# A fused two-block transformer kernel: the mLSTM takes the two heads of a pair together, with a score bank each, and the dense products beside the mixers keep to two banks

## The reference, cut to what matters

```
h = rmsnorm(x, norm1_g[l])
u = jnp.einsum('btd,de->bte', h, w_in[l])
(mq, mk, mv, mo, mi, mf, aq, ak, av, hq, hf, hi, hg) = jnp.split(u, split_at, axis=-1)
y_m = mlstm_mixer(mq, mk, mv, mo, mi, mf, mlstm_conv_w[l], mlstm_gate_b[l], mlstm_norm_g[l])
y_a = diff_attention(aq, ak, av, diff_q_norm_g[l], diff_k_norm_g[l], diff_lambda[l], diff_subln_g[l], lambda_init)
y_h = hgrn2_mixer(hq, hf, hi, hg, lower_bounds[l], hgrn_norm_g[l])
mix = jnp.concatenate([y_m, y_a, y_h], axis=-1).astype(x.dtype)
x = x + jnp.einsum('bte,ed->btd', mix, w_out[l])
```

```
S = jnp.einsum('bhtd,bhsd->bhts', qb, kb) * jnp.exp(D - m_t[..., None])
num = jnp.einsum('bhts,bhsv->bhtv', S, vb) + scale[..., None] * jnp.einsum('bhvk,bhtk->bhtv', C, qb)
den = jnp.sum(S, axis=-1) + scale * jnp.einsum('bhk,bhtk->bht', n, qb)
h = num / jnp.maximum(jnp.abs(den), jnp.exp(-m_t))[..., None]
```

## Time and profile before

| | us |
|---|---|
| median of three runs | 3792.15 |
| lowest and highest | 3792.1, 3793.68 |
| the profiled execution | 3790.01 |
| its span, first to last instruction | 3788.7 |
| mean granted TensorE clock | 0.934 of full |
| PE busy | 3443.1 (91%) |
| DVE, ACT, POOL busy | 1360.0, 1133.6, 1221.5 |

### The profile page before, as it was taken

How to read it: one execution, slowest core, us unless ns; L and a number is a source line. 1 busy time by engine, 2 the same in 40 slices (tenths; PEclk the granted TensorE clock), 3 DMA queues, 4 the chain that set the end, 5 groups by cost and what they waited for, 6 DMA issues and landing times.

```text
span 3788.7 us, 36989 instructions
## 1 busy us (share of the span) xinstructions
PE 3443.1 (91%) x15506; PEld 2733.4 (72%) x15506; DVE 1360.0 (36%) x2212; ACT 1133.6 (30%) x1553; POOL 1221.5 (32%) x300
## 2 busy tenths in 40 slices
PE   7887899998976999999997789998999979769998
PEld 5654588886744788888886678886888857547887
DVE  4437531314257421222126541224221253573123
ACT  2234342322134332322222232223222233422222
POOL 4210044443200244434442234443444431014442
PEclk9887799999978899999998899999999989869998
DMA  3110033332200133333332223323433322013332
GB/s 121 60 52 1 12 100 100 93 96 68 78 19 1 56 100 93 96 100 89 101 86 73 86 67 92 108 89 111 125 93 106 84 97 84 1 39 91 98 96 71
DMA packets 462182, 296.75 MB, mean 78 GB/s; under 512 B 14330, under 2 KB 454192, under 8 KB 462016
## 3 DMA queue, kind: packets, MB, share of 16 engines
q1 hardware_dynamic: 453664, 277.09, 25.0%
q10 hardware_dynamic: 8352, 17.30, 1.3%
HBM read 285.97 MB, written 8.39 MB: 78 GB/s over the span
## 4 chain that ended last, share of the span: by engine, by line
PE 82%; DVE 14%; ACT 3%; issue 1%; POOL 0%; SPq 0%; DMA 0%; ACTq 0%; DVEq 0%
PE bank L473 24%; PE bank L474 24%; PE bank L475 24%; PE bank L313 9%; DVE ta L525 1%; DVE x L750 1%; DVE ta L748 1%; DVE ta L1132 1%; DVE xl L773 1%; DVE qkv L1914 0%; DVE u L1428 0%; DVE ta L1911 0%; DVE scr L1669 0%; DVE sqacc L767 0%; DVE tb L1912 0%
## 5 line engine op out<-in xcount | busy, mean ns | idle before, releaser
L413 POOL TENSOR_TENSOR wlo<-raw,whi 128x2048 fp32r<-128x2048 f32 (+3 forms) x288 | 1209.1, 4199 | 2530.0 <-ACT whi L406 2530.0
L473 PE MATMUL bank<-xh,whi 128*128 128x512 f32 x2432 | 973.6, 400 | 70.4 <-DVE xl L773 39.4
L474 PE MATMUL bank<-xl,whi 128*128 128x512 f32 x2432 | 960.0, 395 | 0.0
L475 PE MATMUL bank<-xh,wlo 128*128 128x512 f32 x2432 | 959.3, 394 | 0.0
L406 ACT ACTIVATE whi<-raw 128x2048 fp32r<-128x2048 f32 (+3 forms) x288 | 503.5, 1748 | 685.6 <-PE bank L475 650.7
L473 PEld LDWEIGHTS bank<-xh,whi 128*128 128x128 f32 x2432 | 465.1, 191 | 187.1 <-POOL wlo L413 33.2
L475 PEld LDWEIGHTS bank<-xh,wlo 128*128 128x128 f32 x2432 | 464.4, 191 | 99.2
L474 PEld LDWEIGHTS bank<-xl,whi 128*128 128x128 f32 x2432 | 465.6, 191 | 93.8
L473 PE MATMUL bank<-ah,whi 128*128 128x512 f32 x1216 | 473.0, 389 | 0.0
L474 PE MATMUL bank<-al,whi 128*128 128x512 f32 x1216 | 473.0, 389 | 0.0
L475 PE MATMUL bank<-ah,wlo 128*128 128x512 f32 x1216 | 473.0, 389 | 0.0
(11 more groups left out here) (333 smaller groups left out, 3046.1 us busy)
## 6 DMA issues: line engine op xcount, KB each, us to landing
raw<-in_ffn_w_gate SPq DMA_DIRECT2D x88, 512.0 KB, 4.0
raw<-in_ffn_w_up SPq DMA_DIRECT2D x88, 512.0 KB, 5.2
raw<-in_w_up SPq DMA_DIRECT2D x64, 512.0 KB, 4.7
raw<-in_w_down SPq DMA_DIRECT2D x64, 512.0 KB, 5.2
raw<-in_w_in SPq DMA_DIRECT2D x56, 512.0 KB, 4.7
raw<-in_ffn_w_down SPq DMA_DIRECT2D x64, 384.0 KB, 4.1
raw<-in_ffn_w_down SPq DMA_DIRECT2D x64, 320.0 KB, 3.7
raw<-in_w_out SPq DMA_DIRECT2D x16, 512.0 KB, 4.4
```

The costliest lines, as they stand in the source:

```text
L413: g.e.tensor_tensor(self.wlo[slot][:, 0:n], self.raw[slot][:, 0:n], self.whi[slot][:, 0:n].bitcast(F32), ALU.subtract).then_inc(self.lo_ma ...
L473: pe.e.matmul(bank, hi[:, at:at + P], xh, start=k == ks[0], stop=False)
L474: pe.e.matmul(bank, hi[:, at:at + P], xl, start=False, stop=False)
L475: last = pe.e.matmul(bank, lo[:, at:at + P], xh, start=False, stop=k == ks[-1])
```

## The change

In the mLSTM the two heads of a pair are taken together. Both `weigh`s of the pair run first; then each b step makes the score blocks of both heads in turn (one on rows 0 to 63 of the array, one on rows 64 to 127) into a bank each (2 and 4), DVE multiplies both, and TensorE sums both. The number of products, of DVE operations and of exponentials stays as it was; the number of steps of the line falls. Nothing of the next pair's `weigh` runs ahead any more. Since bank 2 is now the mLSTM's, the dense units of `in_ah` and `out` all use banks 0 and 1, and TensorE waits, before it begins a bank, until DVE has taken the previous unit's tile out of it. The first unit of each `up` phase also waits for the tiles of the unit before it. hgrn always has banks 0 and 1, `heads(0)` banks 2, 3 and 4.

```diff
+    def two_banks(self, ph):
+        return ph.name.startswith("in_ah") or ph.name.startswith("out")
+
+    def dense_banks(self, u):
+        return 0 if self.two_banks(UNITS[u]) else 2 * (u % 2)
...
+            if u and ph.name.startswith("up") and j == 0:
+                pe.wait_ge(self.tile_read, self.tile_read[u - 1])
...
+                if k == ks[0] and self.two_banks(ph):
+
+                    pe.wait_ge(self.tile_read, self.tile_read[(u - 1, t) if UNITS[u - 1].tiles else u - 1])
                 at = k * w + t * P
-                bank = self.bank[2 * slot + t][:]
+                bank = self.bank[banks + t][:]
...
-        s_bank, row_bank, *sum_banks = [self.bank[b] for b in (4, 5, 6, 7)]
+        row_bank, s_banks, sum_banks = self.bank[5], [self.bank[b] for b in (2, 4)], [self.bank[b] for b in (6, 7)]
...
             elif h == 2:
-                pe.wait_ge(a, a["weights", l, 1])
+                pe.wait_ge(a, a["below", l, 0])
             else:
-                pe.wait_ge(a, a["tokens", l, h // 2])
+                pe.wait_ge(a, a["weights", l, h - 1])
...
             for j in range(b + 1):
-                last = self.mm(s_bank[:, j * P:j * P + P], self.u[part, MK + i, j * P:j * P + P],
-                               self.u[part, MQ + i, b * P:b * P + P], j == 0, j == b)
-            last.then_inc(done.tick("scores", l, h, b), 1)
-        run(weigh(0))
+                for e in range(2):
+                    part = slice(e * HD, e * HD + HD)
+                    last = self.mm(s_banks[e][:, j * P:j * P + P], self.u[part, MK + i, j * P:j * P + P],
+                                   self.u[part, MQ + i, b * P:b * P + P], j == 0, j == b)
+            last.then_inc(done.tick("scores", l, i, b), 1)
         for i in range(2):
             vt = sp(8), sp(9)
-            pe.wait_ge(a, a["below", l, 0] if i else a["weights", l, 0])
+            if i:
+                yield
+            yield from weigh(2 * i)
+            yield from weigh(2 * i + 1)
+            pe.wait_ge(a, a["weights", l, 2 * i + 1])
...
+            scores(i, 0)
+            yield
+            for b in range(NB):
+                yield
+                if b + 1 < NB:
+                    scores(i, b + 1)
...
-            yield from hgrn((mine, mine + 1))
+            yield from hgrn((0, 1))
...
-            yield from weave((heads(0, (2 - mine, 3 - mine, 4)), 1), (line, 1))
+            yield from weave((heads(0, (2, 3, 4)), 1), (line, 1))
```

More of the change, by code:

```diff
@@ L440, in pe_dense @@
         for j in range(ph.count):
-            u, slot = ph.first + j, (ph.first + j) % 2
+            u, slot, banks = ph.first + j, (ph.first + j) % 2, self.dense_banks(ph.first + j)
             pe.wait_ge(self.lo_made, self.lo_made[u])
@@ L453, in pe_dense @@
             if ph.tiles == 0:
-                bank = self.bank[2 * slot]
+                bank = self.bank[banks]
                 for k in range(KC):
@@ L555, in dve_dense @@
                 read = self.tile_read.tick(u, t)
-                self.dve_tile(ph, j, t, self.bank[2 * (u % 2) + t], read)
+                self.dve_tile(ph, j, t, self.bank[self.dense_banks(u) + t], read)
             self.tile_read.tick(u, by=0)
@@ L1047, in pe_mlstm @@
             last.then_inc(done.tick("tokens", l, i), 1)
+            pe.wait_ge(a, a["qk", l, 2 + i])
+            scores(i, 0)
             yield
[L1049 to L1065 removed]
+            for b in range(NB):
+                yield
+                if b + 1 < NB:
+                    scores(i, b + 1)
+                if b == 0:
+                    pe.wait_ge(a, a["tokens", l, i])
+                    pe.wait_ge(v, v["ones", l])
+                    if i:
+                        pe.wait_ge(v, v["out", l, 0])
+                pe.wait_ge(v, v["weighted", l, i, b])
+                for e in range(2):
                     for j in range(b + 1):
[L1067 removed]
                         first, final = b == 0 and j == 0, b == NB - 1 and j == b
[L1069 to L1074 removed]
+                        last = self.mm(sum_banks[e][:, b * P:b * P + P], vt[e][:, j * P:j * P + P],
+                                       weights[e][:, j, b * P:b * P + P], first, final)
+                last.then_inc(done.tick("sums", l, i, b), 1)
+                yield
             self.mm(row_bank[:], self.sel[0:4, i, :], r2).then_inc(done.tick("below", l, i), 1)
[L1076 removed]
             yield
@@ L1143, in weigh @@
             yield
-        run(weigh(0))
         for i in range(2):
+            yield from weigh(2 * i)
+            yield from weigh(2 * i + 1)
             yield
-            for e in range(2):
-                h, wt = 2 * i + e, weights[e]
-                ahead = weigh(h + 1) if h < 3 else iter(())
-                yield
-                v.wait_ge(a, a["weights", l, h])
-                for b in range(NB):
-                    view = wt[:, 0:b + 1, b * P:b * P + P]
-                    v.wait_ge(pe, pe["scores", l, h, b])
-                    v.e.scalar_tensor_tensor(view, s_bank[:, 0:(b + 1) * P].rearrange("p (j t) -> p j t", t=P), HD ** -0.5, view,
-                                             ALU.mult, ALU.mult).then_inc(done.tick("weighted", l, h, b), 1)
-                    yield
-                    next(ahead, None)
-                    yield
-                run(ahead)
+            v.wait_ge(a, a["weights", l, 2 * i + 1])
+            for b in range(NB):
+                v.wait_ge(pe, pe["scores", l, i, b])
+                for e in range(2):
+                    view = weights[e][:, 0:b + 1, b * P:b * P + P]
+                    last = v.e.scalar_tensor_tensor(view, s_banks[e][:, 0:(b + 1) * P].rearrange("p (j t) -> p j t", t=P), HD ** -0.5, view,
+                                                    ALU.mult, ALU.mult)
+                last.then_inc(done.tick("weighted", l, i, b), 1)
+                yield
+                yield
             yield
@@ L1212, in weigh @@
             last.then_inc(done.tick("weights", l, h), 1)
-        run(weigh(0))
         for i in range(2):
+            yield from weigh(2 * i)
+            yield from weigh(2 * i + 1)
+            if i:
+                a.wait_ge(pe, pe["sums", l, 0, NB - 1])
             a.wait_ge(pe, pe["tokens", l, i])
-            if i:
-                a.wait_ge(pe, pe["sums", l, 1, NB - 1])
             for e in range(2):
@@ L1222, in act_mlstm @@
             yield
-            for e in range(2):
-                ahead = weigh(2 * i + e + 1) if 2 * i + e < 3 else iter(())
+            for b in range(NB):
                 yield
-                for b in range(NB):
-                    yield
-                    next(ahead, None)
-                    yield
-                run(ahead)
+                yield
             yield
@@ L2100, in mixers @@
         first = PHASES[f"in_ah{l}"].first
-        mine = 2 * ((first + PHASES[f"in_ah{l}"].count) % 2)
         self.diff_begun = False
```

38 lines of the change are left out of this document (6 added, 32 removed).

## The result

The changed kernel takes **3817.21 us** (median; 3816.14 to 3818.13), where the kernel before takes 3792.12: 25.1 us more, a ratio of 1.0068 with an interval of 1.0055 to 1.008. The forecast was 3790.5, with a range to 3808. The profiled execution has a span of 3816.8 us against 3788.7.

The account below looks back on a forecast made before the run. TensorE bounds the dense stretch; behind it, chains between engines set the pace. Terms from dense stretch through pairs, `out` and `up` sum to -0.8 us a layer, -1.6 in two: 3788.4 profiled, 3790.5 median; own range 3780 to 3800, with rivals 3769 to 3808.

Parts of the forecast that it names:

- the first pair: First head pair: six hgrn levels beside it in both orders, so 77.9 us as now.
- the way to the pairs: From the last dense chunk to the head pairs: 15.8 us where it took 48.7.
- the clock term of the dense stretch: Dense stretch: work lost at half clock behind gaps at two places, 1.7 us more, between 0 and 5.6.
- the price of a level in the second pair: Second head pair: four further hgrn levels at 3.9 us each, 15.6 us more.
- Idle time in the dense stretch: TensorE's waits in the dense stretch: 17.8 us against 9.1, so 8.7 more, bounds 4 and 17.
- The slower rival: ACT's order: roundings delay exponentials, clock falls after each gap, plus DVE hold; 7.6 us a layer, 3805.7 us, chance 0.25.
- Alternation: mLSTM score products alternating halves and banks: 0.145 us each instead of 0.27, 40 products, 5.0 us less on TensorE.
- DVE beside POOL: Gate operations L1258 and L1261 held by POOL's subtraction: 2.0 us a layer, up to 5.0, kept out of the sum.
- Second pair: Second head pair with seven hgrn levels beside it and its end before `out`: 88.5 us for 69.3, bounds 77.9 and 94.
- The rival that levels are hidden: Second pair: the four further levels fall into DVE's idle time, pair takes 77.9 us; kernel 3769.3 us, chance 0.30.
- `out`, `up`: First unit of `out` 13.4 us for 18.6; new wait of 1.0 at each `up`, 1.9 a layer.
- The 2.1 us that the forecast put on for the median: Whole kernel: median of the runs taken 2.1 us above the profiled execution, 3788.4 to 3790.5.

Follow-up runs that it names:

- experiment 3: Changed kernel with throwaway products ahead of the five longest waits of the dense stretch: 3796.19 us, 21.0 less than the change.
- experiment 2: Changed kernel with a step's score products run all for head 0, then all for head 1, not alternating: 3814.91 us.
- experiment 1: Kernel before with the bank part of the change alone, the mLSTM as before: 3797.95 us, ratio 1.0017.
- experiment 7: Kernel before with throwaway products ahead of its waits, 34 in the 9.0 us gap, also in the pairs and ahead of `out`: 3763.28 us, ratio 0.9925.
- experiment 11: Changed kernel with three of hgrn's seven levels in its second tile, the last four left out: 3784.08 us, 33.1 less.
- experiment 15: Changed kernel with throwaway products in all places, in their smaller number, and without the waits at `up`: 3778.24 us.
- experiment 9: Kernel before with throwaway products in the dense stretch and up to the head pairs alone: 3782.94 us, 8.7 less.
- experiment 4: Changed kernel with four steps in place of two in each `weigh` on all engines: 3796.61 us, 20.6 less.
- experiment 14: Kernel before with larger numbers of throwaway products up to the head pairs, smaller ones in them and ahead of `out`: 3756.76 us, ratio 0.9908.
- experiment 5: Changed kernel with throwaway products in the dense stretch, ahead of the gates' columns and `out`, and in the head pairs: 3781.6 us.

## Why the prediction was wrong, point by point

At the start of `out` the first layer is 18.0 us behind the forecast (463.0 for 445.0). Of these, 8.1 came by the end of the chunks (270.9 for 262.8), 5.9 in the first pair and 4.4 in the second; the way to the pairs gave 0.4 back. The step that failed first is the clock term of the dense stretch; the first pair, put at no change, and the price of a level in the second pair failed too.

**Idle time in the dense stretch: right in sum, in part by luck.** 17.3 us for 17.8, from single waits that are off both ways. The wait for L581 is 2.37 (2.4), those ahead of `top` 3.91 and 3.29 (3.9 and 3.95). The wait for the squares of the mLSTM's norm is 4.5 (2.5), the transposes' 0.7 and 1.4 (1.05 and 1.85).

**The clock: the term that failed.** I took 1.7 us "between 0 and 5.6 (twice the row)". Time lost to the clock in a busy stretch can be estimated as its length times one less the mean clock: 148.0 x 0.06 = 8.9 us before, 172.1 x 0.10 = 17.2 after, so 8.3 more. The rows of the falls say about the same: TensorE was busy in them for 8.2, 6.3, 3.2 and 6.6 us, nearly all at half clock, so some 12 us are lost in place of 2.8. My own rows had the price, 2.8 us behind a gap of 9.0; what I mis-judged is that waits of 3.3 to 4.5 us draw falls of the same kind as one of 9.0: four falls in place of one. Experiment 3 leaves the order as it is, takes three of the four away, and ends the dense stretch 8.0 us earlier (262.9 for 270.9). The slower rival had this mechanism, and its sign came true (three falls or more); it priced only two falls and kept the pairs at their length, so its 3805.7 was too small as well.

**Alternation: right in kind, too large.** 2.8 us a layer by experiment 2, not 5.0. The clock's 6.6 over the term and this 2.2, less 0.5 of idle time, are 8.3: the end of the chunks, 8.1 us late, is accounted for.

**DVE beside POOL: real, and left out of the sum.** The changed kernel:

```profile
245.97 4.56 POOL L413 TENSOR_TENSOR wlo<-raw,whi 128x2048 fp32r<-128x2048 f32 x1 [8.07 <-ACT whi L406]
...
247.94 3.15 DVE L1258 TENSOR_TENSOR u<-u 128x512 f32<-128x512 f32 x1 [0.78 <-ACT u L1248]
...
253.24 0.69 DVE L1258 TENSOR_TENSOR u<-u 128x512 f32<-128x512 f32 x1
```

The same operation takes 3.15 us beside the subtraction and 0.69 without it, a hold of 2.46 where 2.0 was put; it ends some 0.6 us behind the subtraction. It reads both its tensors from SBUF, and for this case the Trainium skill (GPSIMD Engine Reference, section 1. Specifications) states contention between DVE and GpSimd. This trace agrees with it. No run here isolates what it costs the whole.

**To the head pairs: right.** 15.4 us for 15.8.

**First pair: the statement that nothing changes was wrong.** TensorE issues the same and its idle time is about the same (77.9 - 55.5 = 22.4, 83.8 - 61.9 = 21.9); it is busy 6.4 us longer, at a clock of 0.68 and not 0.74. On DVE the change's pair has two more of hgrn's copies L1669 (14 for 12, 0.7 us each), which the forecast missed. In the order of the change the length goes with the clock: unfilled, 83.8 us at 0.68, 82.4 at 0.71 and 78.3 at 0.74 (experiment 3, both layers). In the order of before it hardly does: 79.5 us at 0.68 (experiment 1), 77.9 at 0.74, 77.8 at 0.79 (experiment 7). So the low clock alone doesn't explain 83.8 us, and how the 5.9 us divide stays open. Why the clock is lower stays open too: in both kernels TensorE enters the pair at 0.50 and has it for some 13 us; before, it was at 1.00 until 4 us ahead of the pair, now it is at 0.50 from 11 us ahead.

**Second pair: right in its mechanism, the price of a level too small.** Within the pair four levels cost 22.0 us (experiment 11), 5.5 each, where 15.6 and 3.9 were put; that is 6.4 more, and covers the 4.4 us by which the pair came out too long. The rival that levels are hidden is refuted. With fills in both kernels the pair is 29.4 us longer than before, not 19.2 (experiments 7 and 15); why is not resolved.

**`out`, `up`: right.** 12.7 us for 13.4; the wait at the first `up` is 1.0, and all four are worth 3.9 for 3.8. They guard nothing in three of four places.

**The sum.** Of 25.1 us, 12.3 are what fills up to the pairs give back beyond what they give back before (experiments 3 and 9), and some of that lies in the first pair of the second layer; 6.2 are the banks, measured in the order of before (experiment 1, with the 3.9 at `up` in them). If these add, which no run shows, 6.6 are left for the rest, the pairs above all, and are not split. The second layer's first pair in experiment 3 and the first pair in experiment 2 show that what is gained or lost ahead of the pairs changes their length too. The 2.1 us that the forecast put on for the median were scatter: here the profiled execution lies 0.9 above the median.

## What to carry to other kernels

A wait of TensorE can cost its own length and then what the engine loses at half clock behind it. Here that was some 2 to 4 us for each of three waits of 3.3 to 4.5 us, and 2.8 for one of 9.0; so count the waits that a reordering opens, not only their sum. Where such a wait can't be removed, products into an unused bank that end before the wait does hold the clock. They gained 35 us in the kernel before; the change took 10 us longer with the larger numbers of them than with the smaller. When two runs gain the same, look where: experiments 3 and 4 gain 21 us each in different stretches. Work moved from one stretch under another is a gain only if the engine that paces the new place has room: a busy share of 67% on DVE did not mean that four more steps in its chain were free.

## What the runs showed of the hardware

- Inside waits of 3.3, 3.9 and 4.5 us the granted clock fell to 0.50 just as inside one of 9.0 us, for 3 to 10 us. A wait needn't be that long: it also fell 2.6 us after a wait of 1.37 us (change, 247.8 us) and 2.4 us after the same wait in experiment 3 (240.0 us). It stayed at 1.00 behind one of 0.69 us (231.9 us in the change).
- Products of bf16 raise the clock, with a stationary operand of zeros too: 0.99 in the dense stretch of experiment 14 for 0.94 before, and, with zeros, 0.92 for 0.72 in the second pair (experiments 7 and 9).
- Products of 64 rows that alternate between the halves of the array and two banks start every 0.136 us, on one half every 0.205 us (experiment 2).
- The same order of instructions can settle at different clocks in the two layers of one execution: 0.84 and 0.75 in experiment 5, 8 us apart in a pair.
- A DVE operation with two operands in SBUF took 3.15 us beside a subtraction of POOL and 0.69 without it.
